# Last expert's rows into the first token tiles from SBUF: one-hot products on TensorE, other sums on GpSimd

## Chip, cores and metric

The kernel runs on one core of one Trainium2 chip. The metric is the device time of one execution in microseconds (us); the lower the better.

## What is computed

A decoder trunk of two layers over 512 tokens of width 1024, in float32. Layer 0: stick-breaking attention, a dense SwiGLU, LayerNorms, a gated embedding. Layer 1: forgetting attention, then a SwiGLU with 8 experts of which each token uses 2, a LayerNorm, and the gated embedding. The part around the change is the end of layer 1:

```python
top_val, top_idx = lax.top_k(x @ w_router, 2)          # per token
gates = softmax(top_val)
ff = sum over e of gate[e] * swiglu(x, w_gu[e], w_down[e])
x = layer_norm(DEEPNORM_ALPHA * x + ff, g, b)
out = x + (p @ w_proj) * sigmoid(x @ w_gate)
```

## The kernel before, in words

Matrix products are done to float32 precision with three float32r products: each operand is split into a high part (a cast, mostly ScalarE) and a low part (full minus high, VectorE), and `mm3` multiplies high by high, low by high and high by low. Weights come as chunks through SyncE into `ring` (the first four of its six slots are `raw`); ScalarE writes `w_hi`, VectorE `w_lo` (line 1797).

**Experts.** A loop over 8 experts on every engine. For each, GpSimd gathers the rows of its tokens from `x_dram` (indirect DMA), TensorE turns them and multiplies 12 chunks of weights: 0 to 7 give the hidden layer, 8 to 11 the output rows. Rows are worked in slot tiles of 128; the branches of `by_tiles` are for 1, 2 or up to 4 tiles (with two, the second may be half full). ScalarE copies the output rows from PSUM to `y_tok` (L1708). GpSimd's `store_rows` scatters them to `y_dram` (L744) by the slot list: a token's row for its first expert goes to row t, for its second to row 512+t. Chunks 12 to 14 of the last round are already gate weights.

**After the experts.** For each of four token tiles t: SyncE reads both rows back (`y_one`, `y_two`, L660 and L661) and for t > 0 the residual `x_back` (L663); ScalarE scales it (`scale_x`, L1770); VectorE's `combine` adds g_one*y_one and the residual (L2338), then g_two*y_two with the row sums (L2342), and centres (L2346); `gain` (L2351); ScalarE's `spread` gives the variance (L1747, L1750); `finish_norm` writes the normed x in two halves (L2361); TensorE turns it (`turn_x3`, L1290); ScalarE and VectorE write its high and low parts (`turned3_high` L1758, `turned3_low` L1825); TensorE multiplies by the eight gate chunks; ScalarE takes the sigmoid (L1764); VectorE multiplies, adds (`output`, L2374, L2376); SyncE stores. TensorE turns tile t+1 ahead of the last gate chunk of tile t. Gate chunks 3 to 7 are split by `gate_high` and `gate_low`.

**What sets the order.** Each engine runs its own list in the order written, with semaphore waits. SyncE loads six gate chunks (`load_gate`), then `g_row` and `b_row` (L654), then waits until the last scatter has landed (`y_stored`) and issues the rows of tile 0, gate chunks 6 and 7, the rows of tile 1, and, when tile 0 has been turned, those of tiles 2 and 3. VectorE: gate_low(3), (4), (5), combine(0), gain(0), finish_norm(0), turned3_low(0), combine(1), gate_low(6), gain(1), finish_norm(1), gate_low(7), combine(2), turned3_low(1) and so on. GpSimd ends with the scatter of the last expert.

## Time and profile before

| | us |
|---|---|
| median of 3 runs | 1316.58 (1313.56 to 1320.18) |
| the profiled execution | 1314.12 |
| its span | 1312.4 |
| TensorE busy in the span | 1242.6 |
| last expert ends on TensorE, about | 1240.5 |
| first gate product | 1259.91 |
| last output addition starts | 1309.29 |

Times in rows count from the start of the span. A row of a timeline gives start, duration, engine, line, operation and what it wrote and read; in brackets the idle time of the engine before it and what ended it. "x3" means that three instructions are merged into the row. Engines are PE (TensorE), DVE (VectorE), ACT (ScalarE), POOL (GpSimd), SP (SyncE); a name with q is its queue of issues. The chain of waits follows the work that ended last back from the end: each piece was released by the one before it. "issue" is time in which an engine waited for nothing that the profile shows.

### The profile page before, as it was taken

The numbers are of one execution on the slowest core, as the hardware profiler recorded it, in microseconds if no ns is written. First come the engines' busy times: TensorE is split into PE (matmuls) and PEld (weight loads), VectorE is DVE, ScalarE is ACT, GpSimd is POOL, SyncE is SP. The second block draws the span as 40 slices with busy tenths as digits, with TensorE's granted clock in tenths as the row PEclk, the third lists the DMA queues.
The fourth block names the chain that finished last, engine by engine and source line by source line (L and its number), as shares of the span: only waits on it lengthen the run. The fifth ranks groups of instructions, "written<-read, shape, count | busy, mean of one in ns | idle before, by whom it ended". The sixth has DMA issues, their size and how long they took to land.

```text
span 1312.4 us, 16779 instructions
## 1 busy us (share of the span) xinstructions
PE 1242.6 (95%) x6093; PEld 1032.3 (79%) x6094; DVE 654.5 (50%) x857; ACT 538.4 (41%) x723; POOL 53.5 (4%) x67
## 2 busy tenths in 40 slices
PE   7999999999999999999999999999978899999768
PEld 6889998578888887887678789987667788877557
DVE  5334544633333332322753345535575676677874
ACT  3225442442233322111632223322665565676742
POOL 0000000000000000000000000000001211131000
PEclk9999999999999999999999999999988999999979
DMA  6331122323333333330334653122397697789851
GB/s 194 97 97 49 49 65 60 101 80 96 96 96 97 97 115 107 92 88 21 111 93 87 67 100 50 49 82 71 108 332 250 207 331 238 250 294 323 286 225 56
DMA packets 199015, 174.12 MB, mean 133 GB/s; under 512 B 7601, under 2 KB 163313, under 8 KB 198961
## 3 DMA queue, kind: packets, MB, share of 16 engines
q1 hardware_dynamic: 195264, 160.01, 41.6%
q0 software_dynamic: 3120, 11.27, 2.3%
q10 hardware_dynamic: 576, 2.10, 0.4%
q8 instruction: 36, 0.59, 0.2%
q14 instruction: 19, 0.15, 0.0%
HBM read 164.19 MB, written 9.18 MB: 132 GB/s over the span
## 4 chain that ended last, share of the span: by engine, by line
PE 85%; DVE 5%; issue 3%; ACT 3%; DMA 3%; ACTq 0%; SPq 0%; DVEq 0%; POOLq 0%
PE bank L775 25%; PE bank L776 25%; PE bank L777 25%; DMA raw<-moe_w_down 2%; PE bank L1163 2%; PE bank L1164 2%; DVE w_lo L1797 2%; PE bank L869 1%; PE bank L1205 1%; PE bank L1139 1%; DVE x_exact L1915 1%; ACT w_hi L1650 1%; PE bank L1092 1%; PE bank L958 0%; PE bank L962 0%
## 5 line engine op out<-in xcount | busy, mean ns | idle before, releaser
L1797 DVE TENSOR_TENSOR w_lo<-raw,w_hi 128x1024 fp32r<-128x1024 f32 (+4 forms) x212 | 289.7, 1377 | 182.9 <-ACT w_hi L1321 131.4
L775 PE MATMUL bank<-x_hi,w_hi 128*128 128x512 f32 x672 | 264.6, 394 | 11.5 <-DVE w_lo L1797 4.5
L777 PE MATMUL bank<-x_hi,w_lo 128*128 128x512 f32 x672 | 262.7, 391 | 0.0
L776 PE MATMUL bank<-x_lo,w_hi 128*128 128x512 f32 x672 | 262.6, 391 | 0.0
L1321 ACT CAST w_hi<-raw 128x1024 fp32r<-128x1024 f32 (+3 forms) x133 | 143.1, 1076 | 214.5 <-PE bank L777 214.5
L775 PEld LDWEIGHTS bank<-x_hi,w_hi 128*128 128x128 f32 x672 | 126.8, 189 | 44.1 <-DVE w_lo L1797 7.3
L775 PE MATMUL bank<-w_hi,x_hi 128*128 128x256 f32 (+2 forms) x448 | 148.9, 332 | 12.5 <-issue 6.7
L777 PEld LDWEIGHTS bank<-x_hi,w_lo 128*128 128x128 f32 x672 | 126.7, 189 | 26.5
L776 PEld LDWEIGHTS bank<-x_lo,w_hi 128*128 128x128 f32 x672 | 126.7, 189 | 25.6
L776 PE MATMUL bank<-w_lo,x_hi 128*128 128x256 f32 (+2 forms) x448 | 146.1, 326 | 0.0
L777 PE MATMUL bank<-w_hi,x_lo 128*128 128x256 f32 (+2 forms) x448 | 146.1, 326 | 0.0
L1650 ACT CAST w_hi<-raw 128x1536 fp32r<-128x1536 f32 x66 | 93.7, 1423 | 29.2 <-issue 8.2
L775 PEld LDWEIGHTS bank<-w_hi,x_hi 128*128 128x128 f32 x448 | 86.9, 194 | 20.4 <-issue 14.8
L776 PEld LDWEIGHTS bank<-w_lo,x_hi 128*128 128x128 f32 x448 | 87.0, 194 | 5.4
L777 PEld LDWEIGHTS bank<-w_hi,x_lo 128*128 128x128 f32 x448 | 86.7, 194 | 5.4
L775 PE MATMUL bank<-h_hi,w_hi 128*128 128x512 f32 x176 | 68.6, 390 | 3.2 <-DVE h_lo L1797 3.2
L776 PE MATMUL bank<-h_lo,w_hi 128*128 128x512 f32 x176 | 68.5, 389 | 0.0
L777 PE MATMUL bank<-h_hi,w_lo 128*128 128x512 f32 x176 | 68.5, 389 | 0.0
L1797 DVE TENSOR_TENSOR w_lo<-ring,w_hi 128x1536 fp32r<-128x1536 f32 (+1 forms) x32 | 51.4, 1622 | 17.3 <-ACT w_hi L1650 17.3
L1854 DVE SCALAR_TENSOR_TENSOR x_exact<-x_exact,bank 128x512 f32<-128x512 f32 x24 | 16.5, 688 | 82.4 <-PE bank L777 82.4
L2038 DVE TENSOR_TENSOR h_tmp<-h_tmp,bank 128x512 f32<-128x512 f32 x22 | 15.1, 688 | 81.8 <-ACT h_tmp L1542 81.8
L1542 ACT ACTIVATE h_tmp<-bank 128x512 f32<-128x512 f32 x22 | 13.2, 600 | 91.0 <-PE bank L777 91.0
(344 smaller groups left out, 1873.7 us busy)
## 6 DMA issues: line engine op xcount, KB each, us to landing
raw<-ffn_w_gu SPq DMA_DIRECT2D x44, 512.0 KB, 3.8
raw<-moe_w_gu SPq DMA_DIRECT2D x24, 768.0 KB, 7.2
raw<-a_w_qkv SPq DMA_DIRECT2D x24, 512.0 KB, 3.8
raw<-moe_w_gu SPq DMA_DIRECT2D x32, 384.0 KB, 6.0
raw<-moe_w_down SPq DMA_DIRECT2D x16, 768.0 KB, 7.4
raw<-ffn_w_down SPq DMA_DIRECT2D x16, 704.0 KB, 4.5
raw<-kvf_w SPq DMA_DIRECT2D x16, 512.0 KB, 6.7
ring<-moe_w_down SPq DMA_DIRECT2D x16, 512.0 KB
```

Source lines behind the costliest of these rows:

```text
L775: pe.matmul(o, s_hi, m_hi, start=start, stop=False, skip_group_check=True)
L776: pe.matmul(o, s_hi, m_lo, start=False, stop=False, skip_group_check=True)
L777: return pe.matmul(o, s_lo, m_hi, start=False, stop=stop, skip_group_check=True)
L869: pe.matmul(bank[MEAN_BANK[n] + 1][:, :], mean_f[:, :], sq[k % 2][:, :], start=k == 0, stop=k == KD - 1).then_inc(var_done, 1)
L1163: pe.matmul(o, s_both, m_hi, start=start, stop=False, skip_group_check=True)
L1164: return pe.matmul(o, s_both, m_lo, start=False, stop=stop, skip_group_check=True)
L1321: act.copy(w_hi[j % 2][:, 0:n], raw[j][:, 0:n]).then_inc(hi_ready, 1)
L1542: act.activation(h_tmp[j // 2][:, :], bank[j - 1][:, :], ACT.Silu).then_inc(gated, 1)
L1650: act.copy(w_hi[j][:, 0:n], s[:, 0:n]).then_inc(hi_ready, 1)
L1797: return dve.tensor_tensor(dst, a, b, ALU.subtract)
L1854: dve.scalar_tensor_tensor(out=x_exact[:, k, :], in0=x_exact[:, k, :], scalar=ALPHA, in1=psum, op0=ALU.mult, op1=ALU.add).then_inc(summed, 1)
L2038: dve.tensor_tensor(t[:, :], t[:, :], bank[j][:, :], ALU.mult).then_inc(hidden, 1)
```

## The change

- GpSimd fills one row tile with zeros at the start, and two DMAs of ScalarE at the start of the dense layer write it over all 1024 rows of `y_dram`. SyncE waits for them ahead of the chunks of `ffn_w_down`, GpSimd ahead of its expert loop.
- GpSimd works out, for each slot of the last expert, its token (`last_token`), and for each token its gate for that expert (`last_gate`, zero where it is not chosen). When chunk 7 of the last expert is done, it writes a one-hot tile of 128 slots by 256 tokens for each of the four slot tiles (`hot`), in columns of `x_hi` that are free.
- The rows of tile 0 are loaded from `y_dram` when the rows of the first seven experts have landed, ahead of the gate chunks; those of tile 1 when the last product of the last expert is done. Where a token's row belongs to the last expert, the load reads zeros.
- GpSimd (`add_rows`) sums the residual and the two gated rows for tiles 0 and 1, in four instructions each. It scatters the last expert's rows between the two, since tiles 2 and 3 are read back as before (`combine`).
- TensorE (`last_rows`) multiplies the one-hot tiles with `y_tok`, in float32, into two banks for each of the tiles 0 and 1. VectorE (`add_last`) adds last_gate times the bank in two halves, with a row sum of each.
- VectorE's gate_low(3) to gate_low(5) come behind turned3_low(0), gate_low(7) ahead of finish_norm(1). On ScalarE the table load comes first, spread(0) behind gate_high(3), and gate_high(5) behind scale_x(1). SyncE loads gate chunks 6 and 7 behind the rows of tile 1 and ahead of its wait for `y_stored`.
- `y_one`, `y_two` and `x_back` are single tiles at other addresses.

```diff
@@ -330,14 +333,15 @@
-        y_one = at("y_one", [P, TT, D], F32, G + 16 * KB)
-        y_two = at("y_two", [P, TT, D], F32, G + 32 * KB)
-        row_stats = at("row_stats", [P, 5, TT], F32, G + 92 * KB + 672)
+        y_one = [at(f"y_one{t}", [P, D], F32, G + (60, 28, 16, 40)[t] * KB) for t in range(TT)]
+        y_two = [at(f"y_two{t}", [P, D], F32, G + (64, 32, 20, 44)[t] * KB) for t in range(TT)]
+        row_stats = at("row_stats", [P, 6, TT], F32, G + 92 * KB + 672)
+        last_hot = at("last_hot", [P, KD, SEQ], F32, work0)
...
-        x_back = [at(f"x_back{t}", [P, D], F32, (x_mem + 12 * KB, y_mem, y_mem + 4 * KB, G + 60 * KB)[t]) for t in range(TT)]
+        x_back = [at(f"x_back{t}", [P, D], F32, (x_mem + 12 * KB, G + 36 * KB, G + 24 * KB, G + 48 * KB)[t]) for t in range(TT)]
...
@@ -584,6 +600,7 @@
             quads(sp_eng, "gu", gu_step)
+            sp_eng.wait_ge(y_zeroed, 32)
             quads(sp_eng, "down", down_step)
...
@@ -645,30 +662,33 @@
+            def load_rows(t):
+                sp_eng.dma_start(y_one[t][:, :], y_dram[t * P:(t + 1) * P, :]).then_inc(y_first_loaded[t], 16)
+                sp_eng.dma_start(y_two[t][:, :], y_dram[SEQ + t * P:SEQ + (t + 1) * P, :]).then_inc(y_loaded[t], 16)
+                if t:
+                    sp_eng.dma_start(x_back[t][:, :], x_dram[t * P:(t + 1) * P, :]).then_inc(x_returned[t], 16)
+            sp_eng.wait_ge(y_stored, 16 * TT * (NE - 1))
+            sp_eng.wait_ge(xg_turned, TT * NE)
+            load_rows(0)
             for c in range(SLOTS):
                 load_gate(c)
-            sp_eng.wait_ge(xg_turned, TT * NE + TT)
             sp_eng.wait_ge(xg_turned, TT * NE + TT)
...
             sp_eng.wait_ge(rows_stored, 16 * TT)
+            sp_eng.wait_ge(chunk_done, L0 + 12 * NE)
+            load_rows(1)
+            load_gate(6)
+            load_gate(7)
             sp_eng.wait_ge(y_stored, 16 * TT * NE)
-            for t in range(TT):
-                if t == 2:
-                    sp_eng.wait_ge(x3_turned, 2)
-                sp_eng.dma_start(y_one[:, t, :], y_dram[t * P:(t + 1) * P, :]).then_inc(y_first_loaded[t], 16)
-                sp_eng.dma_start(y_two[:, t, :], y_dram[SEQ + t * P:SEQ + (t + 1) * P, :]).then_inc(y_loaded[t], 16)
-                if t:
-                    sp_eng.dma_start(x_back[t][:, :], x_dram[t * P:(t + 1) * P, :]).then_inc(x_returned[t], 16)
-                if t == 0:
-                    load_gate(6)
-                    load_gate(7)
+            load_rows(2)
+            load_rows(3)
             for t in range(TT):
...
                     sp_eng.wait_ge(out_ready, 2 * t + h + 1)
-                    sp_eng.dma_start(out.rearrange("b (t p) d -> (b p) t d", p=P)[:, t, f], y_one[:, t, f]).then_inc(out_stored, 16)
+                    sp_eng.dma_start(out.rearrange("b (t p) d -> (b p) t d", p=P)[:, t, f], y_one[t][:, f]).then_inc(out_stored, 16)
             sp_eng.wait_ge(out_stored, 16 * 2 * TT)
...
@@ -759,15 +780,52 @@
             gather(1, 1)
+            last = slice((NE - 1) * TT, NE * TT)
+            pool.tensor_tensor(last_token[:, :], past[0][:, last], place_c[:, last], ALU.add).then_inc(hot_step, 1)
+            pool.wait_ge(gate_step, 3)
+            for c, g in enumerate((g_one, g_two)):
+                pool.tensor_scalar(gate_pick[:, c, :], top_f[:, :, c], float(NE - 1), None, ALU.is_equal).then_inc(gate_picked, 1)
+            pool.wait_ge(gate_picked, 2)
+            for c, g in enumerate((g_one, g_two)):
+                pool.tensor_tensor(gate_pick[:, c, :], gate_pick[:, c, :], g[:, :], ALU.mult).then_inc(gate_picked, 1)
+            pool.wait_ge(gate_picked, 4)
+            pool.tensor_tensor(last_gate[:, :], gate_pick[:, 0, :], gate_pick[:, 1, :], ALU.add).then_inc(gate_picked, 1)
+            pool.wait_ge(y_zeroed, 32)
             with nc.Fori(0, NE - 1, engines=[pool.engine], hint_back_edge=True, head_slot={pool.engine: 0}) as e:
...
                 pool.nop().then_inc(y_free, 1)
+            pool.nop().then_inc(y_free, 1)
+            pool.wait_ge(chunk_done, L0 + 12 * (NE - 1) + 8)
+            for t in range(TT):
+                pool.iota(hot(t), pattern=[[1, 2 * P]], base=0, channel_multiplier=0,
+                          allow_small_or_imprecise_dtypes=True).then_inc(hot_step, 1)
+                pool.wait_ge(hot_step, t + 2)
+                pool.tensor_scalar(hot(t), hot(t), last_token[:, t:t + 1], None, ALU.is_equal).then_inc(hot_ready, 1)
+            def add_rows(t):
+                pool.wait_ge(y_first_loaded[t], 16)
+                pool.wait_ge(x_scaled, t + 1)
+                pool.tensor_scalar(y_one[t][:, :], y_one[t][:, :], g_one[:, t:t + 1], None, ALU.mult).then_inc(early_added, 1)
+                pool.wait_ge(early_added, 4 * t + 1)
+                pool.tensor_tensor(y_one[t][:, :], y_one[t][:, :], x_back[t][:, :], ALU.add).then_inc(early_added, 1)
+                pool.wait_ge(y_loaded[t], 16)
+                pool.tensor_scalar(y_two[t][:, :], y_two[t][:, :], g_two[:, t:t + 1], None, ALU.mult).then_inc(early_added, 1)
+                pool.wait_ge(early_added, 4 * t + 3)
+                pool.tensor_tensor(y_two[t][:, :], y_two[t][:, :], y_one[t][:, :], ALU.add).then_inc(early_added, 1)
+            add_rows(0)
+            pool.wait_ge(y_first_loaded[1], 16)
+            pool.wait_ge(y_loaded[1], 16)
+            pool.wait_ge(last_spread, 4)
             store_rows(NE - 1, 2 * NE)
+            add_rows(1)
             pool.wait_ge(y_stored, 16 * TT * NE)
-            pool.nop().then_inc(y_free, 1)
         @block.tensor
...
@@ -1280,7 +1338,30 @@
-            pe.wait_ge(banks_out, 8 + 8 * NE)
+            def last_rows(n):
+                for t in range(2):
+                    for h in range(2):
+                        f, o, s = slice(h * 512, (h + 1) * 512), bank[4 + 2 * t + h][:, :], slice(t * P, (t + 1) * P)
+                        if t == h == 0:
+                            pe.wait_ge(hot_ready, TT)
+                            pe.wait_ge(banks_out, 8 * NE + (4 if n <= 2 else 8))
+                        elif t == 0:
+                            pe.wait_ge(banks_out, 8 * NE + 8)
+                        elif h == 0:
+                            pe.wait_ge(xg_ready, TT * NE + TT)
+                        if n == 2:
+                            pe.matmul(o, hot(0)[:, s], y_tok[0][:, f], start=True, stop=False, skip_group_check=True)
+                            pe.matmul(o, hot(1)[0:HALF, s], y_tok[1][0:HALF, f], start=False, stop=False, skip_group_check=True)
+                            mm = pe.matmul(o, hot(1)[0:HALF, s], y_rest[:, 2 * h:2 * h + 2, :], start=False, stop=True, skip_group_check=True)
+                        else:
+                            for i in range(n):
+                                mm = pe.matmul(o, hot(i)[:, s], y_tok[i][:, f], start=i == 0, stop=i == n - 1, skip_group_check=True)
+                        mm.then_inc(last_spread, 1)
+            by_tiles(pe, count(NE - 1), last_rows)
             def turn_x3(t):
...
@@ -1542,6 +1623,10 @@
                 act.copy(h_hi[:, m, :], h_tmp[j // 2][:, :]).then_inc(out_hi, 2)
+            act.wait_ge(zero_set, 1)
+            for h in range(2):
+                act.dma_start(y_dram[0:2 * SEQ, h * 512:(h + 1) * 512].rearrange("(n p) d -> p n d", p=P),
+                              y_zero.rearrange("p (n d) -> p n d", n=1).to_broadcast([P, 2 * TT, SEQ])).then_inc(y_zeroed, 16)
             quads(act, "gu", gu_step, peel=True)
...
@@ -1769,13 +1854,13 @@
+            act.preload_act_table_set("sqrt_and_others")
...
+            spread(0)
...
-            gate_high(5)
-            act.preload_act_table_set("sqrt_and_others")
-            spread(0)
...
+            gate_high(5)
...
@@ -2335,20 +2420,34 @@
-                dve.scalar_tensor_tensor(out=y_one[:, t, :], in0=y_one[:, t, :], scalar=g_one[:, t:t + 1],
+                dve.scalar_tensor_tensor(out=y_one[t][:, :], in0=y_one[t][:, :], scalar=g_one[:, t:t + 1],
...
-                dve.wait_ge(first_added, t + 1)
+                dve.wait_ge(first_added, t - 1)
...
-                dve.scalar_tensor_tensor(out=y_two[:, t, :], in0=y_two[:, t, :], scalar=g_two[:, t:t + 1],
-                                         in1=y_one[:, t, :], op0=ALU.mult, op1=ALU.add, accum_out=row_stats[:, 0, t:t + 1]
+                dve.scalar_tensor_tensor(out=y_two[t][:, :], in0=y_two[t][:, :], scalar=g_two[:, t:t + 1],
+                                         in1=y_one[t][:, :], op0=ALU.mult, op1=ALU.add, accum_out=row_stats[:, 0, t:t + 1]
...
-                dve.wait_ge(second_added, t + 1)
+                dve.wait_ge(second_added, t - 1)
...
+            def add_last(t):
+                dve.wait_ge(early_added, 4 * t + 4)
+                dve.wait_ge(gate_picked, 5)
+                for h in range(2):
+                    f = slice(h * 512, (h + 1) * 512)
+                    dve.wait_ge(last_spread, 2 * t + h + 1)
+                    dve.scalar_tensor_tensor(out=y_two[t][:, f], in0=bank[4 + 2 * t + h][:, :], scalar=last_gate[:, t:t + 1],
+                                             in1=y_two[t][:, f], op0=ALU.mult, op1=ALU.add,
+                                             accum_out=row_stats[:, 5 * h, t:t + 1]).then_inc(last_added, 1)
+                dve.wait_ge(last_added, 2 * t + 2)
+                dve.tensor_scalar(row_stats[:, 1, t:t + 1], row_stats[:, 0, t:t + 1], row_stats[:, 5, t:t + 1], -1.0 / D,
+                                  ALU.add, ALU.mult).then_inc(centre_ready, 1)
...
-                dve.scalar_tensor_tensor(out=y_one[:, t, :], in0=y_two[:, t, :], scalar=row_stats[:, 1, t:t + 1],
+                dve.scalar_tensor_tensor(out=y_one[t][:, :], in0=y_two[t][:, :], scalar=row_stats[:, 1, t:t + 1],
...
@@ -2371,23 +2470,23 @@
...
+            dve.wait_ge(rows_loaded, 32)
+            add_last(0)
+            gain(0)
+            finish_norm(0)
+            turned3_low(0)
             gate_low(3)
...
             gate_low(5)
-            dve.wait_ge(rows_loaded, 32)
-            combine(0)
-            gain(0)
-            finish_norm(0)
-            turned3_low(0)
-            combine(1)
             gate_low(6)
+            add_last(1)
             gain(1)
+            gate_low(7)
             finish_norm(1)
-            gate_low(7)
             combine(2)
```

## Rows read from the trace of the kernel before

**Rows 1.** The page, busy time of each engine.
```profile
PE 1242.6 (95%) x6093; PEld 1032.3 (79%) x6094; DVE 654.5 (50%) x857; ACT 538.4 (41%) x723; POOL 53.5 (4%) x67
```

**Rows 2.** Table of stretches; (x) instructions, then granted clock, DMA share, GB/s.
```profile
1208.00:1240.60 32.60, 30.24 (x140) 24.48 (x140) 26.31 (x22) 23.99 (x26) 3.55 (x5) 1.00 0.97 323
1240.60:1260.00 19.40, 2.03 (x9) 1.69 (x9) 11.67 (x15) 7.51 (x11) 2.03 (x1) 0.55 0.58 223
1260.00:1310.00 50.00, 47.90 (x216) 39.39 (x216) 33.54 (x49) 20.68 (x31) 0.00 (x0) 0.97 0.27 101
```

**Rows 3.** The chain of waits, 1243 to 1262: start, us, what.
```profile
1243.59 2.31 DMA y_dram<-y_tok,store_i
1245.90 5.83 issue
...
1253.11 1.30 DVE y_two L2342 x2
...
1257.33 1.10 PE bank L1290 x4
...
1259.91 0.77 PE bank L775
...
1261.95 0.43 PE bank L776
```

**Rows 4.** Timeline of SyncE: start, us, what.
```profile
1222.66 6.79 SPq L646 DMA_DIRECT2D raw<-ple_w_gate  x4
...
1248.05 0.33 SPq L660 DMA_DIRECT2D y_one<-y_dram  x1
```

**Rows 5.** Timeline of TensorE, the turn to token tile 1.
```profile
1270.95 1.03 PE L1290 MATMUL bank<-ident,y_two 128*128 128x128 f32 x8
...
1273.21 0.40 PE L775 MATMUL bank<-w_hi,turned_hi 128*128 128x512 f32 x1
```

**Rows 6.** Groups of TensorE with shapes: count | busy, mean ns | idle before.
```profile
L1092 PE MATMUL bank<-x_exact,w_r 128*8 128x512 f32 x16 | 7.0, 593 | 0.2 <-ACT x_exact L1402 0.2
```

**Rows 7.** Groups of GpSimd with shapes.
```profile
L737 POOL TENSOR_TENSOR y_tok<-y_tok,y_part 64x1024 f32<-64x1024 f32 x3 | 7.2, 2397 | 15.4 <-issue 15.4
...
L691 POOL TENSOR_SCALAR_AFFINE_SELECT ident<-ident 128x128 f32<-128x128 f32 x1 | 0.3, 287 | 0.2 <-POOL clip_b L680 0.2
...
L706 POOL IOTA spare<- 128x1 f32 x1 | 0.1, 133 | 0.0
```

**Rows 8.** Timeline of GpSimd in three experts.
```profile
1109.76 0.86 POOL L749 COPY store_i<-place_i 128x4 int32 x1
...
1156.81 2.40 POOL L737 TENSOR_TENSOR y_tok<-y_tok,y_part 64x1024 f32<-64x1024 f32 x1 [6.27 <-issue]
...
1224.18 0.19 POOL L749 COPY store_i<-place_i 128x4 int32<-128x4 int32 x1 [7.30 <-DMA y_dram<-y_tok,store_i]
```

**Rows 9.** Timeline of VectorE at the same places.
```profile
1108.81 1.75 DVE L1797 TENSOR_TENSOR w_lo<-raw,w_hi 128x1536 fp32r<-128x1536 f32 x1
...
1157.69 3.14 DVE L1797 TENSOR_TENSOR w_lo<-raw,w_hi 128x1536 fp32r<-128x1536 f32 x1 [3.19 <-ACT w_hi L1650]
```

**Rows 10.** Timeline of ScalarE: chunk 7 of the last expert, and scale_x(1).
```profile
1230.21 0.33 ACT L1687 ACTIVATE he<-bank 128x192 f32<-128x192 f32 x1
...
1259.79 1.07 ACT L1770 ACTIVATE x_back<-x_back 128x1024 f32<-128x1024 f32 x1
```

**Rows 11.** Timeline of VectorE in the last expert.
```profile
1230.12 1.76 DVE L1797 TENSOR_TENSOR w_lo<-ring,w_hi 128x1536 fp32r<-128x1536 f32 x1 [0.51 <-ACT w_hi L1650]
...
1232.46 1.76 DVE L1797 TENSOR_TENSOR w_lo<-ring,w_hi 128x1536 fp32r<-128x1536 f32 x1 [0.32 <-ACT w_hi L1650]
...
1237.95 5.69 DVE L1797 TENSOR_TENSOR w_lo<-raw,w_hi 128x1536 fp32r<-128x1536 f32 x4
```

**Rows 12.** DMA issues, 1236.1 to 1237: KB, us to landing.
```profile
b_row<-ln_b SPq DMA_DIRECT2D x1, 512.0 KB, 6.3
```

**Rows 13.** Groups of VectorE with shapes, 1240 to 1312.
```profile
L1797 DVE TENSOR_TENSOR gate_lo<-ring,gate_hi 128x1024 fp32r<-128x1024 f32 x2 | 2.4, 1218 | 0.0
```

More of the change, by code:

```diff
@@ L274, in build @@
         tiles_f = [sb(f"tiles_f{i}", [P, NE + 1]) for i in range(2)]
+        last_token = sb("last_token", [P, TT])
+        last_gate = sb("last_gate", [P, TT])
+        gate_pick = sb("gate_pick", [P, 2, TT])
         tiles_i = sb("tiles_i", [P, NE + 1], I32)
@@ L351, in build @@
         tail = [raw_mem + (6 * i + 4) * KB for i in range(RAW + 2 * SPLIT)]
+        y_zero = at("y_zero", [P, SEQ], F32, tail[0])
         t_side = at("t_side", [P, SEQ], R32, tail[0])
@@ L462, in build @@
         padded = sem("padded")
+        zero_set = sem("zero_set")
+        y_zeroed = sem("y_zeroed")
+        gate_picked = sem("gate_picked")
+        hot_step = sem("hot_step")
+        hot_ready = sem("hot_ready")
+        early_added = sem("early_added")
+        last_spread = sem("last_spread")
+        last_added = sem("last_added")
         packed_moved = sem("packed_moved")
@@ L511, in flat, with hot @@
             return ring[slot][:, 0:k * n].rearrange("p (k n) -> p k n", k=k)
+        def hot(t):
+            return last_hot[:, (2, 3, 6, 7)[t], 2 * P:SEQ]
         BUILT = 8
@@ L681, in _ @@
             last.then_inc(built, 1)
+            pool.memset(y_zero[:, :], 0.0).then_inc(zero_set, 1)
             pool.wait_ge(built, 1)
@@ L1290, in turn_x3 @@
                         mm = pe.transpose(bank[4 + t % 2 * 2 + h][:, k * P:(k + 1) * P],
-                                          y_two[:, t, (4 * h + k) * P:(4 * h + k + 1) * P], ident[:, :])
+                                          y_two[t][:, (4 * h + k) * P:(4 * h + k + 1) * P], ident[:, :])
                     mm.then_inc(x3_turned, 1)
@@ L1746, in spread @@
                 act.wait_ge(centre_ready, t + 1)
-                act.activation(x_back[t][:, :], y_two[:, t, :], ACT.Square, bias=row_stats[:, 1, t:t + 1],
+                act.activation(x_back[t][:, :], y_two[t][:, :], ACT.Square, bias=row_stats[:, 1, t:t + 1],
                                accum_out=row_stats[:, 2, t:t + 1]).then_inc(spread_ready, 1)
@@ L2214, in read_list @@
                 dve.wait_ge(list_step, 2)
-                dve.tensor_tensor(past[0][:, :], past[0][:, :], past[1][:, :], ALU.add).then_inc(list_step, 1)
+                dve.tensor_tensor(past[1][:, :], past[0][:, :], past[1][:, :], ALU.add).then_inc(list_step, 1)
                 dve.wait_ge(list_step, 3)
-                dve.tensor_tensor(token_i[:, :], past[0][:, :], place_c[:, :], ALU.add).then_inc(list_ready, 1)
+                dve.tensor_tensor(token_i[:, :], past[1][:, :], place_c[:, :], ALU.add).then_inc(list_ready, 1)
             read_list()
@@ L2360, in finish_norm @@
                     f = slice(h * 512, (h + 1) * 512)
-                    dve.scalar_tensor_tensor(out=y_two[:, t, f], in0=y_one[:, t, f], scalar=row_stats[:, 4, t:t + 1],
+                    dve.scalar_tensor_tensor(out=y_two[t][:, f], in0=y_one[t][:, f], scalar=row_stats[:, 4, t:t + 1],
                                              in1=b_row[:, f], op0=ALU.mult, op1=ALU.add).then_inc(x3_ready, 1)
@@ L2373, in output @@
                     dve.wait_ge(sig_ready, 2 * t + h + 1)
-                    dve.tensor_tensor(y_one[:, t, f], x_back[t][:, f], proj_tok[:, t, f], ALU.mult).then_inc(gate_scaled, 1)
+                    dve.tensor_tensor(y_one[t][:, f], x_back[t][:, f], proj_tok[:, t, f], ALU.mult).then_inc(gate_scaled, 1)
                     dve.wait_ge(gate_scaled, 2 * t + h + 1)
-                    dve.tensor_tensor(y_one[:, t, f], y_one[:, t, f], y_two[:, t, f], ALU.add).then_inc(out_ready, 1)
+                    dve.tensor_tensor(y_one[t][:, f], y_one[t][:, f], y_two[t][:, f], ALU.add).then_inc(out_ready, 1)
+            dve.wait_ge(rows_loaded, 32)
[3 more added lines that the diff above has]
+            turned3_low(0)
             gate_low(3)
```

## The prediction

> **What bounds the kernel now.** I read the page first. TensorE is busy for 95% of the span [rows 1], so only a hole in TensorE's row is worth anything. The table of stretches shows where one is: in the last expert's 32.6 us TensorE works 30.2, in the 19.4 us behind it 2.0, and then 47.9 of 50 [rows 2]. The chain of waits through the hole [rows 3] reads: GpSimd's scatter of the last expert's rows (issued at 1243.59), then 5.83 us in which nothing that the profile names is waited for (it holds SyncE's readback, issued at 1248.05 [rows 4]), the second addition of token tile 0 on VectorE at 1253.11, its norm, transposes at 1257.33, and the first gate product at T0 = 1259.91. From there TensorE doesn't stop: tile 1's transposes start at 1270.95 and its gate products at T1 = 1273.21 [rows 5]. What follows T1 is full of gate products and is moved as a whole. So the change is worth what it does to T0 and then to T1.
>
> **Part 1: the first start.** Scatter and readback leave tile 0's path. In their place stand one-hot products on TensorE, four sums on GpSimd (add_rows(0)) and one on VectorE in two halves (add_last(0)). Prices, from the nearest rows:
> - TensorE: a float32 product of 128x512 shows as two records, and 16 records took 7.03 us [rows 6], so 0.88 us a product. The last expert has one scatter [rows 3], so one slot tile, so four products: tile 0's are out at about 1242.4, all at 1244.1.
> - GpSimd, two inputs, 1024 columns: 2.40 us. One input over 1024 columns has no row: at least the fixed cost, 0.13 us (iota of one column), at most the two-input price, 2.4. The affine select over 128 columns took 0.287 [rows 7], so (0.287-0.133)/128 = 1.2 ns a column: 1.4 us for 1024, 0.44 for 256. I take these, the select being the nearest row, and for an iota over 256 columns 0.35 (an estimate between 0.13 and 0.44).
>
> GpSimd and VectorE hold each other up, in both directions. A VectorE split of 128x1536 takes 1.75 us; one that came 0.9 us behind a GpSimd addition took 3.14 and ended at 1160.83, 1.62 us behind the addition's end (1159.21). A 128x4 copy on GpSimd takes 0.19 us; one that came during a split took 0.86 and ended at 1110.62, where the split ended (1110.56) [rows 8, 9]. All three additions in the trace do this to VectorE. So I count both engines' work on SBUF operands as one queue.
>
> The Trainium skill has this as a rule ("SBUF — State Buffer", Who interferes with whom): an exclusive lock between a GpSimd instruction that reads SBUF and a VectorE one with two SBUF inputs. The Trainium skill ("GPSIMD Engine Reference", Engine selection) also calls one-input work on GpSimd roughly line rate; by its clock 1024 columns would be 0.9 us (an estimate from that page), and by that the total below would be about 2 us smaller; no row here shows it.
>
> Now the times. GpSimd may write the one-hot tiles when chunk 7 of the last expert is done, about 1230.2 (ScalarE's use of it is at 1230.21 [rows 10]). Four pairs of 0.35 and 0.44 are 3.2 us; the splits at 1230.12 and 1232.46 [rows 11] hold two of the compares for 3 us together: ready at 1236.5. The first multiplication fits into VectorE's gap and ends at 1237.9. Left are 2.4+1.4+2.4 = 6.2 us on GpSimd and on VectorE three of the splits that began at 1237.95 (four took 5.69 us [rows 11], so 4.5). In one queue, in whatever order: 1237.9+6.2+4.5+0.2 for semaphores = 1248.8. There add_last(0) starts. It takes the place of the addition at 1253.11: 4.3 us gained. Two halves with two accumulator reads cost 0.3 more, so T0 = 1255.9. TensorE has idled for 9 us by then, so the restart is at half clock as before (1.10 us for four transposes, products 0.43 apart [rows 3]): nothing gained there.
>
> Moved ahead of this, and hidden by it: SyncE now waits for expert 6's store and issues 1 MB of row loads ahead of the gate loads, the first of which went out at 1222.66 [rows 4]. The DMA engines are full (share 0.97, 323 GB/s [rows 2]), so what lies behind lands 3.2 us later: b_row at 1245.7 instead of 1242.45 [rows 12]. ScalarE's casts of the gate chunks, and its copies of the expert's rows between them, slip by 1 to 2 us. All that is under 1248.8; were GpSimd fast, b_row would be last (rival B). Clearing y_dram (4 MB, two DMAs of ScalarE at the start of the dense layer) runs beside loads that are four chunks ahead: 0, at most 2 us. The operations on last_gate stand where GpSimd waits for an expert: 0.
>
> **Part 2: tile 1, late next.** GpSimd must issue the scatter first (2.4 us from the rows' copies to its start, 2 us itself: until 1253.5) and then waits for x_scaled, which ScalarE gives behind turned3_high(0): at 1260.86 before [rows 10], T0+0.95, so now 1256.9. Only then come its four sums, 7.6 us with 0.2 between. SyncE's last row loads follow the scatter's issue by 4.5 us (1243.59 to 1248.05), in time. At T0+0.7 = 1256.6 VectorE starts gate_low(3) to gate_low(6), which the change puts behind turned3_low(0): four of 1.22 us [rows 13]. One queue again: 1256.6+7.8+4.9 = 1269.3. Queued behind that on VectorE are add_last(1) 1.6, the centre 0.2, gain(1) 1.3, gate_low(7) 1.2, reciprocal and first half of the norm 0.9: 5.2 us. So tile 1 can be turned at 1274.5. TensorE wants it at T0+11.0 = 1266.9. It stands over 7 us and restarts at half clock: transposes 1.9, the six products of the last gate chunk 2.6, T1 = 1279.0. VectorE's combine(2) and turned3_low(1), 2.7+0.7 behind the second half at 1275.2, end at 1278.7 and don't set it. T1 is 5.8 us late, and the rest of the half-clock stretch costs 0.4: **+6.2 us**.
>
> **The rivals.**
> A, the forecast, +6.2. With a one-input price between 0.9 and 1.8 us (-2.2 to +2.0) and a microsecond either way for what I called hidden: +3 to +9.
> B, faster: the engines don't hold each other up here. For it: the rows show single short meetings; against: none of them is without the wait. One-hot tiles at 1233.6, sums until 1241.3, b_row at 1245.7 decides, T0 = 1245.7+7.1 = 1252.8. Tile 1's sums end at T0+8.8, with the 5.2 behind them tile 1 is turned at 1266.8, and combine(2) and the low parts bring T1 to 1270.9: -2.3 us. It decides as long as GpSimd's second set ends before T0+9.
> C, slower by more: one-input work on GpSimd costs as much as two-input work. Each set grows by 2 us, the one-hot tiles by 0.6: T0 = 1258.5, tile 1 turned at 1279.1, T1 = 1283.6: +10.8 us. It decides from about 1.8 us a sum.
> D, as the change reads: tile 0 starts when its products are out (1242.9, T0 = 1250.0) and tile 1 is never late: -9.9 us. Against it: behind x_scaled at T0+0.95, 7.8+5.2 us would have to fit into 10.
>
> **How the numbers follow.** The profiled execution before took 1314.12 us (span 1312.4), the median is 1316.58. My sums are differences, set on the median: A 1322.8, B 1314.3, C 1327.4, D 1306.7. Chances 0.45, 0.2, 0.2, 0.1, others 0.05. The likeliest is A: 1322.8, alone 1319.6 to 1325.6. The range 1311 to 1329 holds A, B and C with their bounds. 0.5% (6.6 us) is about what a measurement of this kernel can tell from no change; A lies across it (0.26 within, 0.19 above). Faster 0.12, within 0.48, slower 0.40.
>
> **What would show it.** GpSimd's two-input sums at 2.4 us, one-input ones at 1.4 plus waits; VectorE's splits between 1238 and 1249 stretched by whole GpSimd operations; add_last's first row near 1248.8 and gate products from 1255.9; gate_low(3) to (6) stretched; a hole of 7 us in TensorE before tile 1's transposes, ended by VectorE's y_two. The forecast is wrong if the splits keep 1.22 and 1.75 us beside GpSimd's sums (B), if one-input sums take over 1.8 us (C), or if TensorE has no hole before tile 1 (D).

## The result, and the profile after

The changed kernel takes 1331.7 us (median of 5 runs, 1329.04 to 1335.74), before 1316.58 (a median of 5 too, not of the 3 that the table above says): ratio 1.0112, 95% interval 1.0091 to 1.0133. It is slower by 15 us (12 to 17.5). One of the 8 executions of e1 below ran slow, 1800.33 us at a granted clock of 0.652, and is left out of its median and its ratio. The forecast was 1322.8 with a range of 1311 to 1329, so the sign of the likeliest case was right, its size less than half of what came, and the time lies outside the range. The profiled execution has a span of 1328.3 us, 15.9 longer than that of before.

The first reading is the table of stretches of the changed kernel, from 1240.6 on, with an edge put at 1276. Columns: stretch and length, busy time of TensorE, its weight loads, VectorE, ScalarE and GpSimd with (x) instructions, then granted clock, DMA share, GB/s.

```profile
1240.60:1260.00 19.40, 11.26 (x45) 7.37 (x45) 11.55 (x12) 8.75 (x10) 17.46 (x12) 0.87 0.83 305
1260.00:1276.00 16.00, 12.46 (x48) 10.10 (x48) 9.79 (x11) 7.54 (x10) 10.86 (x4) 0.73 0.53 191
1276.00:1310.00 34.00, 26.57 (x115) 21.77 (x114) 24.04 (x38) 14.66 (x22) 3.01 (x2) 0.85 0.17 66
```

Two things differ from [rows 2]. From 1240.6 to 1260, where TensorE had worked 2.0 us, it now works 11.3: the last expert isn't finished at 1240.6. And behind 1276, where before there was no hole, 7.4 of 34 us are idle. TensorE's timeline of the changed kernel puts times to both:

```profile
1248.65 3.74 PE L1361 MATMUL bank<-y_tok,last_hot 128*128 128x512 f32 x8
...
1262.91 1.94 PE L1371 MATMUL bank<-ident,y_two 128*128 128x128 f32 x8 [10.52 <-DVE y_two L2460]
1265.48 0.77 PE L833 MATMUL bank<-w_hi,turned_hi 128*128 128x512 f32 x1 [0.64 <-DVE turned_lo L1910]
...
1284.27 1.94 PE L1371 MATMUL bank<-ident,y_two 128*128 128x128 f32 x8 [7.43 <-DVE y_two L2460]
```

The one-hot products follow the last expert directly, so their start is its end: 1248.65, where before it was 1240.5. That is 8.2 us lost before the part that I had costed. Single executions differ here by some 2 to 3 us by chance: e2, e3 and e8 below, which do the same work until then, have this end at 1242.8, 1241.4 and 1244.7. Counted from that end (E), the events of the tail are:

| us after E | before | forecast | after |
|---|---|---|---|
| start of the addition that the norm follows | 12.6 | 8.3 | 9.8 |
| T0, first gate product | 19.4 | 15.4 | 16.8 |
| tile 1 is turned | 30.4 | 34.0 | 35.6 |
| T1, first gate product of tile 1 | 32.7 | 38.5 | 39.9 |

So the tail costs 7.2 us where I said 5.8 and 0.4 more (+6.2), in the places that I said: T0 is earlier, then a hole of 7.43 us, ended by VectorE's y_two, takes more than it gave. The other half of the loss is elsewhere. GpSimd's timeline of the changed kernel gives the prices:

```profile
1244.67 0.93 POOL L808 TENSOR_SCALAR last_hot<-last_hot,last_token 128x256 f32<-128x256 f32 x1
1245.57 2.87 POOL L814 TENSOR_SCALAR y_one<-y_one,g_one 128x1024 f32<-128x1024 f32 x1
1248.52 3.66 POOL L816 TENSOR_TENSOR y_one<-y_one,x_back 128x1024 f32<-128x1024 f32 x1
1252.16 3.81 POOL L818 TENSOR_SCALAR y_two<-y_two,g_two 128x1024 f32<-128x1024 f32 x1
1256.06 2.34 POOL L820 TENSOR_TENSOR y_two<-y_two,y_one 128x1024 f32<-128x1024 f32 x1
...
1266.61 4.49 POOL L814 TENSOR_SCALAR y_one<-y_one,g_one 128x1024 f32<-128x1024 f32 x1 [4.18 <-ACT x_back L1855]
...
1273.82 2.85 POOL L818 TENSOR_SCALAR y_two<-y_two,g_two 128x1024 f32<-128x1024 f32 x1
1276.75 2.34 POOL L820 TENSOR_TENSOR y_two<-y_two,y_one 128x1024 f32<-128x1024 f32 x1
```

With nothing beside them, a two-input sum of 128x1024 takes 2.34 us, as taken from [rows 7], but a one-input scaling 2.85, not 1.4, and a compare over 256 columns 0.93, not 0.44. VectorE's timeline of the changed kernel shows who stands beside the long ones, and who waits for the last:

```profile
1246.27 7.00 DVE L1882 TENSOR_TENSOR w_lo<-raw,w_hi 128x1536 fp32r<-128x1536 f32 x3
1258.50 0.75 DVE L2441 SCALAR_TENSOR_TENSOR y_two<-bank,last_gate,y_two 128x512 f32<-128x512 f32 x1 [5.23 <-issue]
...
1266.11 1.22 DVE L1882 TENSOR_TENSOR w_lo<-raw,w_hi 128x1024 fp32r<-128x1024 f32 x1
1267.24 3.19 DVE L1882 TENSOR_TENSOR gate_lo<-ring,gate_hi 128x1024 fp32r<-128x1024 f32 x2
1270.36 1.21 DVE L1882 TENSOR_TENSOR gate_lo<-raw,gate_hi 128x1024 fp32r<-128x1024 f32 x1
1279.12 0.75 DVE L2441 SCALAR_TENSOR_TENSOR y_two<-bank,last_gate,y_two 128x512 f32<-128x512 f32 x1 [7.55 <-POOL y_two L820]
```

Both additions of the last expert's rows start when GpSimd's fourth instruction ends (1258.40 and 1279.09).

### The profile page after: what moved, and what is told of

Same layout as the page of the kernel before. It is cut to its first block, busy times and chain, and to the rows that moved or that the text cites. A ratio compares the mean times of both kernels' runs of the same rounds, so it can differ in the third digit from the quotient of the medians.

```text
span 1328.3 us, 16831 instructions
## 1 busy us (share of the span) xinstructions
PE 1254.3 (94%) x6101; PEld 1033.7 (78%) x6102; DVE 654.8 (49%) x859; ACT 538.5 (41%) x723; POOL 87.4 (7%) x90
## 4 chain that ended last, share of the span: by engine, by line
PE 84%; DVE 5%; issue 3%; ACT 3%; POOL 2%; DMA 2%; ACTq 0%; SPq 0%; DVEq 0%; POOLq 0%
PE bank L833 25%; PE bank L834 24%; PE bank L835 24%; PE bank L1222 2%; PE bank L1221 2%; DVE w_lo L1882 2%; PE bank L927 1%; DMA raw<-moe_w_down 1%; PE bank L1263 1%; PE bank L1197 1%; DVE x_exact L2000 1%; ACT w_hi L1735 1%; POOL y_one L814 1%; PE bank L1150 1%; POOL y_one L816 0%
## 5 line engine op out<-in xcount | busy, mean ns | idle before, releaser
L833 PE MATMUL bank<-w_hi,x_hi 128*128 128x256 f32 (+2 forms) x448 | 148.1, 331 | 17.3 <-issue 15.4
```

The lines of the kernel that those rows point to most:

```text
L833: pe.matmul(o, s_hi, m_hi, start=start, stop=False, skip_group_check=True)
```

## The experiments

Line numbers in a row are those of the kernel that it is from. "The addresses of before" means that the large region G, which holds most of the work buffers, starts where it started before.

### Where the 8 us ahead of the tail come from

The change also adds three small tensors, which lie below G:

```diff
+        last_token = sb("last_token", [P, TT])
+        last_gate = sb("last_gate", [P, TT])
+        gate_pick = sb("gate_pick", [P, 2, TT])
```

G is the next free byte, rounded up to 64, so its start goes from byte 130432 of a partition to 130560. Theory 1 was that this, and GpSimd's sums in the tail, are two separate costs; the rivals were contention by something that the change does earlier, and the clearing of y_dram. Five kernels tell them apart.

**e1_pad128**: the kernel before, and nothing but an unused tensor.

```diff
+        pad = sb("pad", [P, 24])
         G = (place[0] + 63) // 64 * 64
```

> The kernel before with one unused tensor that moves all the large tiles behind it 128 bytes up, as the three small tensors of the change do; nothing else differs. Theory 1 (the early loss of 8.3 us comes from the new addresses of the tiles: products spaced 232 instead of 227 ns where the moving operand lies in them): 4 to 6 us slower than before, median near 1321.5, spacing of 232 ns in the o0, down and o1 phases. Theory 2 (clearing y_dram and the code around it cost the early time): within 1 us of before, spacing 227 ns everywhere.

1323.26 us (median of seven), ratio 1.0046 (1.0027 to 1.0065): an unused tensor costs 6.1 us (3.6 to 8.6), at the upper end of what I had expected. The trace shows where. This is one of TensorE's groups from 860 to 945 us (the output projection of the second attention; count | busy, mean ns), first of before and then of e1:

```profile
L776 PE MATMUL bank<-q_lo,w_hi 128*128 128x512 f32 x64 | 24.9, 389 | 0.0
```

```profile
L777 PE MATMUL bank<-q_lo,w_hi 128*128 128x512 f32 x64 | 25.3, 395 | 0.0
```

The same products, with no idle time ahead of them in either kernel, are 6 ns longer, and their starts are that much further apart. The changed kernel has 395 too. Three stages show it in all their products, those whose moving operand (the one of 512 columns, here q or h) lies at G: 192, 528 and 192 products. 912 by 5.5 to 6.2 ns (by duration, and from start to start) is 5.0 to 5.7 us. Products whose moving operand is x, whose buffer lies below G and isn't moved, keep their pace. From 260 to 480 us, of before and of e1:

```profile
L776 PE MATMUL bank<-x_lo,w_hi 128*128 128x512 f32 x322 | 125.3, 389 | 0.0
```

```profile
L777 PE MATMUL bank<-x_lo,w_hi 128*128 128x512 f32 x322 | 125.3, 389 | 0.0
```

So the loss goes with the products whose own moving buffer was moved. The experts' products with w moving, of whose four pairs of buffers two lie at G, show it in part: their starts are 229.5 ns apart on the mean in e1, 227.2 before. The first of the three stages between two fixed events, TensorE's first 512-column product of it and the first of the stage behind, of before and of the changed kernel:

```profile
193.22 0.44 PE L775 MATMUL bank<-q_hi,w_hi 128*128 128x512 f32 x1
...
253.87 0.47 PE L775 MATMUL bank<-x_hi,w_hi 128*128 128x512 f32 x1 [0.83 <-DVE x_lo L1923]
```

```profile
193.02 0.45 PE L833 MATMUL bank<-q_hi,w_hi 128*128 128x512 f32 x1
...
254.87 0.47 PE L833 MATMUL bank<-x_hi,w_hi 128*128 128x512 f32 x1 [0.76 <-DVE x_lo L2008]
```

60.65 us before, 61.85 after.

**e2_same_addresses**: the changed kernel, with the three tensors in free bytes at the end of G, so that G starts at 130432 again.

```diff
-        last_token = sb("last_token", [P, TT])
...
+        last_token = at("last_token", [P, TT], F32, G + 93 * KB + 928)
+        last_gate = at("last_gate", [P, TT], F32, G + 93 * KB + 960)
+        gate_pick = at("gate_pick", [P, 2, TT], F32, G + 93 * KB + 992)
```

> The changed kernel with its three small tensors put into a free corner, so that the large tiles have the addresses of before. Theory 1: 4 to 6 us faster than the changed kernel, so 1325.5 to 1328, and 8 to 11 us slower than before; products 227 ns apart in the o0, down and o1 phases. Theory 2 (clearing): still about 1331.7.

1323.02 us, ratio 1.0037 (1.0019 to 1.0055). The products have 389 and 390 ns again, the last expert ends at 1242.8, and GpSimd's sums are those of the changed kernel. T1 comes at 1282.73, 39.9 after E. This is the change alone, 4.9 us slower (2.5 to 7.2) where I had forecast 6.2. The remaining 0.75% of the 1.12 is the address by this pair, 0.46% in e1; the two agree within the sum of their intervals. But I had expected only 4 to 6 us between e2 and the changed kernel, and it was 8.7 to 9.9 (by the medians and by the ratios), more than 912 products account for.

**e5_pad64** and **e6_pad256**: is any move bad, or only some starts?

e5, with G at 130496:

```diff
+        pad = sb("pad", [P, 16])
```

e6, with G at 130688:

```diff
+        pad = sb("pad", [P, 56])
```

> The kernel before with an unused 64-byte tensor ahead of the large region G, so that every buffer at G starts 64 bytes later (130496, which is 192 above a multiple of 256; before 130432, which is 128 above one; in the changed kernel and with the 128-byte pad 130560, a multiple of 256). Theory 'the start within 256 bytes decides': the 512-column products whose moving operand lies at G start every 227 ns as before or every 232 ns as with the 128-byte pad, by whether 192 belongs to the good or the bad starts; if only multiples of 256 are bad, 227 ns and a span of 1312 to 1316 us. Rival 'the distance between two buffers decides': any move brings 232 ns, in at least one of the three stages, and a span of 1319 to 1322.

> The kernel before with an unused 224-byte tensor ahead of G, so that every buffer at G starts 256 bytes later (130688, again 128 above a multiple of 256), further off than in the changed kernel. Theory 'the start within 256 bytes decides': spacing of 227 ns in all stages, first expert product as early as before (idle ahead of it 3.9 us, not 8.9), span within 2 us of before. Rival 'the distance between two buffers decides' (or the mere presence of another tensor): 232 ns and a span of 1319 to 1322.

Single executions took 1323.09 and 1316.67 us, beside a median of 1317.63 for before. TensorE's groups from 561 to 611 us (the down projection), of e5 and then of e6:

```profile
L777 PE MATMUL bank<-h_lo,w_hi 128*128 128x512 f32 x73 | 28.8, 394 | 0.0
L778 PE MATMUL bank<-h_hi,w_lo 128*128 128x512 f32 x74 | 28.7, 388 | 0.0
L776 PE MATMUL bank<-h_hi,w_hi 128*128 128x512 f32 x73 | 28.6, 392 | 0.0
```

```profile
L777 PE MATMUL bank<-h_lo,w_hi 128*128 128x512 f32 x74 | 28.8, 389 | 0.0
L778 PE MATMUL bank<-h_hi,w_lo 128*128 128x512 f32 x74 | 28.8, 389 | 0.0
L776 PE MATMUL bank<-h_hi,w_hi 128*128 128x512 f32 x74 | 28.8, 389 | 0.0
```

Moved by 256 bytes, twice as far as in the changed kernel, nothing is lost: a tensor more isn't the cause, nor just any move. Moved by 64, the products are slower by part of it. The time of e5 doesn't tell what that costs, since its TensorE also stood 5 us longer ahead of the first expert product (last section). So of four starts two are good (130432 and 130688, both 128 above a multiple of 256), one is bad (130560, a multiple) and one between (130496, 192 above). Why the place inside 256 bytes should matter to a product isn't shown by any run, nor whether it is the place itself or the distance to something that didn't move.

**e4_clearing_alone**: the kernel before, with the zero tile, the two DMAs over y_dram and the waits for them.

```diff
+            pool.memset(y_zero[:, :], 0.0).then_inc(zero_set, 1)
...
+            sp_eng.wait_ge(y_zeroed, 32)
...
+            act.wait_ge(zero_set, 1)
+            for h in range(2):
+                act.dma_start(y_dram[0:2 * SEQ, h * 512:(h + 1) * 512].rearrange("(n p) d -> p n d", p=P),
+                              y_zero.rearrange("p (n d) -> p n d", n=1).to_broadcast([P, 2 * TT, SEQ])).then_inc(y_zeroed, 16)
```

> The kernel before with only the clearing of y_dram and its waits added; the cleared rows are used by nothing. Theory 1 (addresses): within 1 us of before. Theory 2 (clearing costs): 3 to 8 us slower, with the loss behind the start of the dense layer.

1318.37 us, ratio 1.0001 (0.9985 to 1.0018). The clearing costs nothing that can be measured, as costed.

The traces of before and of the changed kernel divide the 8.2 us. At the end of TensorE's work ahead of the expert loop the changed kernel is 6.5 us behind (960.90 against 954.41): 5.0 to 5.7 are the address, and most of the rest is a stretch of 3.4 us at a granted clock of 0.50, from 500.6 on. Every profiled execution but that of before has such a stretch at about 500 us (6.8 us long in e2), so it isn't the change's. The first expert product comes 5.1 us later still (idle for 8.95 us instead of 3.88, last section), and 3.4 us are made up by the last expert's end. So this pair of traces doesn't measure the address alone. The cleanest pair for it is e8 and e10 below: in neither profile is that product late.

### What the tail's loss comes from

**e3_sums_on_vector**: e2, and VectorE does the sums of tiles 0 and 1, in two instructions each, directly ahead of the halves of add_last; GpSimd does none.

```diff
-            add_rows(0)
...
-            add_rows(1)
...
             def add_last(t):
-                dve.wait_ge(early_added, 4 * t + 4)
+                dve.wait_ge(y_first_loaded[t], 16)
+                dve.wait_ge(x_scaled, t + 1)
+                dve.scalar_tensor_tensor(out=y_one[t][:, :], in0=y_one[t][:, :], scalar=g_one[:, t:t + 1],
+                                         in1=x_back[t][:, :], op0=ALU.mult, op1=ALU.add).then_inc(early_added, 1)
+                dve.wait_ge(early_added, 2 * t + 1)
+                dve.wait_ge(y_loaded[t], 16)
+                dve.scalar_tensor_tensor(out=y_two[t][:, :], in0=y_two[t][:, :], scalar=g_two[:, t:t + 1],
+                                         in1=y_one[t][:, :], op0=ALU.mult, op1=ALU.add).then_inc(early_added, 1)
+                dve.wait_ge(early_added, 2 * t + 2)
```

> As the run with the old addresses, but VectorE does the four sums of tiles 0 and 1 in two instructions each (1.28 us), directly ahead of add_last; GpSimd only writes the one-hot tiles and scatters. Theory 1 (GpSimd's sums, 2.3 to 4.5 us each, and the queue between them and VectorE's splits are what makes both starts late): first gate product about 13.5 us behind the last expert's end (16.7 in the changed kernel), tile 1's gate products about 30 us behind it (39.8; 32.7 before), so some 10 us faster than the same kernel with GpSimd's sums and about level with before, 1314 to 1320. Rival (tile 1 is late because of the order on VectorE, the late scale_x and gate_low, whoever sums): only 2 to 4 us faster than it, 1322 to 1325.

1314.72 us, ratio 0.9987 (0.9966 to 1.0008): level with before, and 8.3 us under e2. VectorE's timeline of e3:

```profile
1239.00 4.55 DVE L1869 TENSOR_TENSOR w_lo<-raw,w_hi 128x1536 fp32r<-128x1536 f32 x3
1244.36 1.28 DVE L2425 SCALAR_TENSOR_TENSOR y_one<-y_one,g_one,x_back 128x1024 f32<-128x1024 f32 x1 [0.81 <-DMA b_row<-ln_b]
1245.68 1.28 DVE L2429 SCALAR_TENSOR_TENSOR y_two<-y_two,g_two,y_one 128x1024 f32<-128x1024 f32 x1
1247.00 0.75 DVE L2436 SCALAR_TENSOR_TENSOR y_two<-bank,last_gate,y_two 128x512 f32<-128x512 f32 x1
```

The three splits take 4.55 us instead of 7.00, and what GpSimd did in 12.8 us VectorE does in 2.6. Add_last starts 5.6 us after E instead of 9.8, and the hole ahead of tile 1's transposes shrinks from 6.97 us (e2) to 0.84. T0 comes 12.6 us after E, T1 29.4. The rival, that the order on VectorE made tile 1 late whoever sums, is out: it had 2 to 4 us.

**e7_immediate_scale**: is it the gate column, an operand that changes with the partition, that makes the one-input scaling dear? e2, with the first rows of tiles 0 and 1 scaled by 0.5 instead of their gate; the gate of these rows is left out.

```diff
-                pool.tensor_scalar(y_one[t][:, :], y_one[t][:, :], g_one[:, t:t + 1], None, ALU.mult).then_inc(early_added, 1)
+                pool.tensor_scalar(y_one[t][:, :], y_one[t][:, :], 0.5, None, ALU.mult).then_inc(early_added, 1)
```

> The kernel e2 (the change with its buffers at the addresses of before) in which GpSimd scales the first rows of tiles 0 and 1 by the constant 0.5 instead of the gate column; the second rows keep the gate column. The output is therefore not the reference's. Undisturbed one-input instructions of 128x1024 took 2.84 to 2.87 us with the gate column, the two-input sums 2.34. If the operand that changes with the partition is what makes them dearer than the sums, the constant form takes 1.2 to 2.4 us beside 2.85 for the other; if an f32 instruction with one input costs this much on GpSimd by itself, both forms take 2.8 to 2.9.

GpSimd's timeline of e7:

```profile
1239.10 2.79 POOL L814 TENSOR_SCALAR y_one<-y_one 128x1024 f32<-128x1024 f32 x1
1241.98 3.66 POOL L816 TENSOR_TENSOR y_one<-y_one,x_back 128x1024 f32<-128x1024 f32 x1
1245.61 3.82 POOL L818 TENSOR_SCALAR y_two<-y_two,g_two 128x1024 f32<-128x1024 f32 x1
1249.51 2.34 POOL L820 TENSOR_TENSOR y_two<-y_two,y_one 128x1024 f32<-128x1024 f32 x1
```

The single execution took 1322.95 us. 2.79 us against 2.87 with the column in e2 and in the changed kernel, each beside the first of VectorE's three splits. The column accounts for 0.08 us; the one-input form by itself costs more than the two-input sum.

### A version that beats both

**e8_order_on_vector**: e3, in an order of work that goes by its own trace.

```diff
-            dve.wait_ge(rows_loaded, 32)
             add_last(0)
+            dve.wait_ge(rows_loaded, 32)
             gain(0)
             finish_norm(0)
-            turned3_low(0)
             gate_low(3)
+            turned3_low(0)
...
             gain(1)
-            gate_low(7)
             finish_norm(1)
-            combine(2)
+            gate_low(7)
             turned3_low(1)
+            combine(2)
...
-                        if t == 0:
-                            gate_weights(4 * h + c)
                         if h == 1 and c == 3 and t + 1 < TT:
                             turn_x3(t + 1)
+                        if t == 0:
+                            gate_weights(4 * h + c)
```

> e3 (all sums on VectorE, buffers at the addresses of before) in another order: VectorE's wait for g_row and b_row stands ahead of gain(0) instead of ahead of the sums (-0.8 us), the split of gate weights 3 stands in the 1.23-us wait for ScalarE's copy of the turned rows (-1.2 on what follows), the split of weights 7 stands behind finish_norm(1) and TensorE turns tile 1 before it waits for that split (-1.1 at the turn), and turned3_low(1) stands ahead of the sums of tile 2 (-1.3 at the first product of tile 1, if nothing else is late there). By the theory that VectorE's queue ahead of these four places sets the end: S 0.8 us earlier than in e3, the last products of tile 1 begin 2.5 to 3.5 us earlier, time 1311 to 1313 against before 1317, ratio 0.995 to 0.998. By the rival that gate weights 4 to 7 or the rows of tile 2 come last by then: within 1 us of e3.

1312.0 us, ratio 0.9956 (0.9939 to 0.9973): 5.8 us faster than before (3.6 to 8.0). TensorE's timeline of e8:

```profile
1244.65 3.73 PE L1348 MATMUL bank<-y_tok,last_hot 128*128 128x512 f32 x8
1253.79 1.94 PE L1358 MATMUL bank<-ident,y_two 128*128 128x128 f32 x8 [5.41 <-DVE y_two L2455]
...
1268.68 1.03 PE L1358 MATMUL bank<-ident,y_two 128*128 128x128 f32 x8
...
1270.94 0.40 PE L820 MATMUL bank<-w_hi,turned_hi 128*128 128x512 f32 x1
```

Add_last starts 4.7 us after E, tile 1's transposes have no idle time ahead of them any more, and T1 comes 26.3 us after E, where before it was 32.7. Of the rivals, the late gate weights or rows would have left it within 1 us of e3; it came 4.1 us under it by the ratios (0.5 to 7.7), and T1 comes 3.1 us earlier after E than in e3.

**e9_before_order**: does the order alone do it? The kernel before, with TensorE's turn ahead of its wait for gate weights 7 and turned3_low(1) ahead of combine(2), as in the diff above.

> The kernel before, with only the two steps of e8's order that it can take: TensorE turns tile 1 ahead of its wait for the split of gate weights 7, and turned3_low(1) stands ahead of combine(2). In the kernel before the turning of tile 1 has no idle time ahead of it and VectorE waits 0.71 us ahead of turned3_low(1), so both theories of the rest agree on little: the first product of tile 1 at most 1 us earlier, ratio 0.999 to 1.001. If e8's gain came from the order and not from the one-hot products with the sums on VectorE, this kernel would show it too: ratio 0.995 to 0.997.

1317.79 us, ratio 1.0007 (0.9990 to 1.0023). These two steps give nothing where the scatter and the readback are in tile 0's path; the other steps of e8's order weren't tried there.

**e10_order_pad128**: e8, with e1's unused tensor.

> e8 with a 96-byte tensor ahead of G, so that the region starts at 130560 as in the changed kernel. If address and tail are separate effects that add: spacing 232 ns in the three stages, the last expert's end 6 to 8 us later than in e8, time 6 us above e8, 1318 to 1320, ratio to before 1.000 to 1.002. If the address effect is hidden or the tail absorbs it, within 3 us of e8.

1317.09 us, ratio 1.0005 (0.9986 to 1.0025). The last expert ends at 1252.64 instead of 1244.65, and everything behind it is as far from it as in e8 (first gate product at 11.7 us in both). The two effects add, and the address by itself would have taken all of e8's gain.

## Why the prediction was right or wrong, step by step

**The work ahead of the last expert** was costed at nothing but the clearing and the row loads. For these that holds (e4 for the clearing, and e2, whose last expert ends at 1242.8, between e6's 1242.2 and e4's 1243.3). The step that failed is one that the prediction doesn't have: that the products ahead of the tail keep their pace when buffers move. The change moves them by 128 bytes, and that costs 6.1 us by e1's ratio, 6.5 by the ratios of e10 and e8, and 9.9 by those of the changed kernel and e2, each uncertain by 2.5 to 3.7 us, so they agree. The range's top of 1329 was built from the tail alone. With 6.1 to 6.5 us for the address the forecast of 1322.8 would have been 1328.9 to 1329.3; the tail's 7.2 us in the trace instead of 6.2 is 1.0 more.

**Prices on GpSimd.** Two inputs: right, 2.34 for 2.40. One input: mis-sized, 2.85 for 1.4 us. The affine select, whose row I took as nearest, is another operation and isn't a guide for this one. The bound that I gave, "at most the two-input price", was also broken: the forecast assumed that less input can't take longer, and no row said so. The compares came to 0.93 instead of 0.44. The Trainium skill's remark that one-input work on GpSimd runs at roughly line rate ("GPSIMD Engine Reference", Engine selection), which would be 0.9 us (an estimate from the clock on that page), isn't what this trace shows for float32 scaling either: it took 2.85.

**One queue.** Right for a two-input sum and a split, too strong for a one-input scaling. VectorE's row of 7.00 us in the changed kernel is these three splits:

```profile
1246.27 2.03 DVE L1882 TENSOR_TENSOR w_lo<-raw,w_hi 128x1536 fp32r<-128x1536 f32 x1
...
1248.22 1.75 DVE L1882 TENSOR_TENSOR w_lo<-raw,w_hi 128x1536 fp32r<-128x1536 f32 x1
...
1249.89 3.37 DVE L1882 TENSOR_TENSOR w_lo<-raw,w_hi 128x1024 fp32r<-128x1024 f32 x1
```

The third takes 1.22 us in e3. Here it came during GpSimd's two-input sum and ended at 1253.27, 1.09 us behind the sum's end (1252.18); the sum in turn had come during the second split and took 3.66 us instead of 2.34. That is the taking of turns of [rows 8, 9]. But the first split ran inside the first scaling (1245.57 to 1248.44) and lost 0.28 us, the scaling nothing. In the second set a scaling of 2.85 us took 4.49 (1266.61 to 1271.10), and two VectorE splits began and ended inside it, together 3.19 us long instead of 2.35 in e3. So a one-input scaling can be slowed by splits, but it didn't hold them until its end. Over the first set each engine lost 2.3 to 2.5 us, not the other's whole time. With 2.85 and 0.93 in my own sum, one queue would have put add_last(0) at 1253.4 in the times of before, 12.9 after E; it came 9.8 after. The dearer scaling and the milder hold-up set each other off: the forecast of the tail (6.2) lies within e2's interval by two errors of opposite sign, and that is luck. The Trainium skill's exclusive lock between the two engines ("SBUF — State Buffer", Who interferes with whom) agrees with these rows for the sum and the third split. It makes no exception for a one-input instruction that reads SBUF, and for the scaling the rows don't agree with it.

**Part 1, tile 0.** Gained 2.6 us on T0 in place of 4.0. What is last there is GpSimd's set, as the forecast had it, not b_row: with the sums gone, b_row is what VectorE waits for in e3 (0.81 us), as I said that it would be next.

**Part 2, tile 1.** Right in mechanism: GpSimd waits for x_scaled (4.18 us idle, ended by ScalarE's x_back), its set runs beside gate_low(3) to (6), add_last(1) waits 7.55 us for it, and TensorE has a hole of 7.43 us and restarts at half clock (granted clock 0.50 from 1279 to 1289; transposes in 1.94 us instead of 1.03).

**The rivals.** B (no hold-up) is out. C's condition, over 1.8 us for a scaling, is met, but its +10.8 us isn't: its sum kept the one queue. D, the change as it reads, failed as the prediction said, for want of time on GpSimd; what it promised is to be had on VectorE, and e8 gets 5.8 of its 9.9 us.

## What to carry to other kernels

Work that leaves a path must be cheap where it goes: two VectorE instructions of 1.28 us were replaced here by four GpSimd instructions that took 12.8 us and slowed VectorE as well, and the engine that was relieved then waited for them, 5.2 and 7.6 us. Where an edit adds a tensor, compare the start of every large buffer before and after, and look at the mean duration of one unchanged instruction in a stage that the edit doesn't touch: that one number (389 or 395 ns) pointed at what costs 6 of the 15 us here. And where the nearest row for a price is of another operation, the bound has to reach beyond the dearest row of its kind.

## What the runs showed of the hardware

- The same 128x512 products, with q or h moving, took 389 to 391 ns with their buffers' region at 130432 and 130688, 395 to 397 at 130560, and 388 to 396, unevenly, at 130496 (groups away from stretches at half clock).
- GpSimd, float32, 128x1024: two inputs 2.34 us and one input with a gate column 2.85 with nothing beside them; beside a split of VectorE, one input 2.87 with the column and 2.79 with a constant.
- A split of 128x1024 on VectorE that came during a two-input sum on GpSimd ended 1.09 us behind the sum's end (changed kernel; 1.08 in e7's second set); one that came during a one-input scaling ended before it.
- Left open: TensorE's first expert product came about 5 us late in some executions, with nothing that the profile names ahead of it. The changed kernel, e1, e5, e7 and e9 show 8.5 to 9.0 us of "issue" there (first row below, the changed kernel), the others 3.8 to 3.9 us ended by x_lo (second row, e10). It doesn't follow the address, since e7 and e9 have it at the addresses of before and e10 doesn't have it at the changed ones, and since e10 loses as much as e1 without it, the loss by the address doesn't need it. Part of it is made up: from that product to the last expert's end it is 276.9 to 282.1 us in the five and 280.1 to 285.0 in the other seven, and a wait for VectorE's he, 15 to 18 us behind that product, is 0.5 us in the five and 1.7 to 2.7 in the others. What it is, and what it costs at the end, wasn't settled.

```profile
969.85 0.79 PE L833 MATMUL bank<-w_hi,x_hi 128*128 128x512 f32 x1 [8.95 <-issue]
```

```profile
967.60 0.79 PE L821 MATMUL bank<-w_hi,x_hi 128*128 128x512 f32 x1 [3.91 <-DVE x_lo L1898]
```
